# RWKV-7 scan on one core: paired state factors, a block-diagonal state copy, and the inverse scaled on ScalarE

## The chip, the cores and the metric

The program runs on one core of a Trainium2 chip. The metric is the device time of one execution in microseconds. TensorE (PE in the profile, its weight loads PEld) multiplies, VectorE (DVE) and ScalarE (ACT) work on its results, GpSimd (POOL) has little to do here, and SyncE (SP) issues the DMAs. Each engine works through its own instruction queue in order and waits at semaphores for the others.

## The reference, cut to what matters

The program is one layer of a hybrid block: modulated norm, two token mixers side by side (RWKV-7 and GLA), a merge, and a SwiGLU feed-forward part. The change touches the RWKV-7 recurrence alone. It has 16 heads of width 64, 256 context tokens followed by 256 latent tokens, and it runs forward and backward over them; an output is wanted for latent tokens only.

```python
def step(s, inp):                      # s: (heads, v, k), one token
    w_t, k_t, v_t, kk_t, a_t = inp[:5]
    sa = jnp.einsum('bhvk,bhk->bhv', s, kk_t)
    s = (s * w_t[:, :, None, :] - sa[..., None] * (kk_t * a_t)[:, :, None, :]
         + v_t[..., None] * k_t[:, :, None, :])
    return s, jnp.einsum('bhvk,bhk->bhv', s, r_t)     # output, latent tokens only
```

## The kernel before, in words

The scan (phase_rwkv_scan, L1228) works in chunks of C = 64 tokens. There are 8 chunks (NCH) in each of the two directions, and one chunk c in one direction d is called a half here: HALVES lists them as (0,f), (0,b), (1,f), (1,b), and so on, 16 in all, numbered 0 to 15. Halves 0 to 7 are context, 8 to 15 latent. A tile of 128 partitions by 8 pairs (U8) by 64 columns holds all 16 heads, two heads to a pair, one in each half of the partitions.

Within a chunk the recurrence becomes small matrix products per head:

- Decays: a cumulative sum b (DVE, "prepare", L1438), its exponentials es and e2 (ACT, L1543 and L1548), and from them the scaled factors: the two state factors in ldr[:, 1:3] (DVE, "prepare1", L1444), q1 and q2 in q12 (L1452, L1460).
- Scores: products of factors to N (pb, "scores1", L1641), T2 and R2 (pa, L1652), R1 (pb, L1658), each masked on DVE (first L1479, t2r2 L1485, r1 L1490).
- The inverse of (1 - N): five doublings. Each is a DVE transpose (L1463), a DVE mask product (L1465, "step"), an ACT copy ("grown", L1577) and 16 products on PE ("grow", L1694). It ends with "close" (ACT copy L1583, two DVE transposes to "cross" L1499), the product "inverse" (PE L1703), and on DVE L1511, xt = 0.5 * product + half_eye.
- Turning by PE: V to tokens first (L1666, copy vt on ACT L1567), the two state factors (L1666 twice, copies s1t L1571 and s2t L1573).
- own_part (T2 times V, L1711) and rhs_sum (plus q1 times the state S, L1719), copied by ACT (L1587); u = inverse times rhs (L1726, copy L1591).
- Output, latent only: q2 times the state (from_state, L1734), plus R2 times V (L1744), plus R1 times U (L1747).
- State: S + s2^T V + s1^T U (PE L1758 and L1760, 64 x 64 products), added and scaled on DVE (L1519, L1522).

Each fp32 product of the program appears as two matmul records and two weight loads in the trace, so a group of 16 heads is "x32" there. A turning is one record each.

The order on every engine is written out by hand in run(step), L1344. In pass n it interleaves three halves: "now" (half n), "lev" (half n - 1) and "last" (half n - 2). PE's order in a pass is: grow 0 of lev, rhs of last, grow 1, u and from_state of last, grow 2, output and state of last, grow 3, scores of now, grow 4, tokens and flips of now, own_part and inverse of lev; then the next pass. DVE has stage 1 of lev as its first work in a pass, "stage l" being the transpose and mask product after grow l - 1. "prepare" of the half ahead stands at the end of a pass in passes 0 to 7, before own_part and inverse, and in the middle (after stage 3) from pass 8. Passes 16 and 17 only drain.

SP's queue loads ldr (768 KB) and kkv (512 KB) for each half, once q1, b and the second turning of the same direction's last chunk are done.

## Time and profile before

| | us |
|---|---|
| Median of three runs (lowest 2246.99, highest 2255.99) | 2254.05 |
| The profiled execution | 2254.09 |
| Its span | 2252.2 |
| The scan in it: from the first decay sum (978.7) to the last output sum (1285.9) | 307 |
| PE busy over the whole span | 2045.4 (91%) |
| DVE busy | 1363.5 (61%) |
| ACT busy | 789.7 (35%) |

The rest of the program is unchanged work before and after the scan, so the scan is where a difference has to arise. The busy shares are of the whole span; in the scan they are lower for PE and higher for DVE, which the windows below show by pass. In a timeline, each line is an instruction or a merged run of them: its start, its length, engine, line, operation, output and inputs, and in brackets how long the engine had been idle before it and who ended that. "issue" there is idle time of an engine that waited for nothing the profile shows. PEclk is the granted TensorE clock as a share of 2.4 GHz, so 1.00 is 2.4 GHz and 0.50 is 1.2 GHz.

### The profile page before, as it was taken

What the parts mean: (1) busy time and instruction counts of PE and PEld (TensorE: products, weight loads), DVE (VectorE), ACT (ScalarE), POOL (GpSimd) and SP (SyncE); (2) the same over time, 40 slices, a digit from 0 to 9 for tenths busy, and PEclk for the clock granted to TensorE, in tenths of its full rate; (3) what the DMA queues carried; (4) which work ended last, traced back from release to release, by engine and by line L of the source; (5) the groups of instructions that cost most, each with busy time, mean ns of one, the idle gap of its engine ahead of it and who ended that gap; (6) DMA issues with size and microseconds to landing.
All of it is one profiled execution on the core that took longest, in us unless ns stands there. A gap on an engine that the chain in (4) does not pass through costs nothing. (4 is left out here: it accounts for less than half of the span.)

```text
span 2252.2 us, 38698 instructions
## 1 busy us (share of the span) xinstructions
PE 2045.4 (91%) x16787; PEld 1684.7 (75%) x16787; DVE 1363.5 (61%) x1287; ACT 789.7 (35%) x858; POOL 275.8 (12%) x135
## 2 busy tenths in 40 slices
PE   7679999999899989966666799989999999999997
PEld 3268888888589867656666688778888888888886
DVE  3465666665438447768877778466565656554444
ACT  1231111113162225524433365344443434333333
POOL 0242213124105214401000020000000000000000
PEclk9589999999899999988999999999999999999998
DMA  9978888886353378986444187545555555555552
GB/s 334 348 272 327 314 308 305 311 310 181 106 155 103 85 210 260 302 189 171 85 85 87 46 192 260 210 132 179 194 187 194 187 187 186 186 199 193 188 200 97
DMA packets 406151, 454.17 MB, mean 202 GB/s; under 512 B 107550, under 2 KB 356750, under 8 KB 388734
## 3 DMA queue, kind: packets, MB, share of 16 engines
q1 hardware_dynamic: 398400, 441.04, 61.3%
q10 hardware_dynamic: 7614, 11.10, 1.3%
q8 instruction: 110, 1.80, 0.3%
q14 instruction: 27, 0.22, 0.0%
HBM read 413.89 MB, written 38.22 MB: 201 GB/s over the span
## 5 line engine op out<-in xcount | busy, mean ns | idle before, releaser
L215 DVE TENSOR_TENSOR f_w_lo<-t_w_raw,f_w_hi 128x2048 fp32r<-128x2048 f32 x132 | 302.5, 2291 | 307.7 <-ACT f_w_hi L209 307.7
L270 PE MATMUL pf<-h,f_w_hi 128*128 128x512 f32 x1320 | 463.9, 395 | 0.0
L209 ACT ACTIVATE f_w_hi<-t_w_raw 128x2048 fp32r<-128x2048 f32 x132 | 253.4, 1920 | 446.3 <-PE pf L270 283.5
L269 PE MATMUL pf<-h,f_w_lo 128*128 128x256 f32 x1320 | 367.4, 278 | 0.3 <-DVE h L2586 0.3
L270 PEld LDWEIGHTS pf<-h,f_w_hi 128*128 128x128 f32 x1320 | 247.6, 188 | 54.3
L269 PEld LDWEIGHTS pf<-h,f_w_lo 128*128 128x128 f32 x1320 | 248.3, 188 | 4.6 <-DVE h L2586 0.6
L209 ACT ACTIVATE p_w_hi<-h_w_raw 128x2048 fp32r<-128x2048 f32 (+1 forms) x52 | 96.4, 1903 | 340.6 <-DVE stage L726 252.1
L261 PE MATMUL p_in<-h,p_w_lo 128*128 128x512 f32 (+1 forms) x512 | 199.3, 389 | 0.0
L259 PE MATMUL p_in<-h,p_w_hi 128*128 128x512 f32 (+1 forms) x512 | 199.3, 389 | 0.0
L260 PE MATMUL p_in<-h,p_w_hi 128*128 128x512 f32 (+1 forms) x512 | 199.2, 389 | 0.0
L2782 PE MATMUL d_out<-f_w_hi,hid 128*128 128x512 f32 x704 | 178.8, 394 | 6.1 <-DVE f_w_lo L215 6.1
L858 DVE SCALAR_TENSOR_TENSOR late_acc<-h_of_x,siluc,late_acc 128x2048 f32<-128x2048 f32 x60 | 160.6, 2676 | 38.7 <-DMA h_of_x<-in_ada_w 37.1
L215 POOL TENSOR_TENSOR p_w_lo<-h_w_raw,p_w_hi 128x2048 fp32r<-128x2048 f32 (+1 forms) x26 | 123.5, 4752 | 314.3 <-ACT p_w_hi L209 314.3
L2782 PEld LDWEIGHTS d_out<-f_w_hi,hid 128*128 128x128 f32 x704 | 133.7, 190 | 34.9 <-DVE f_w_lo L215 6.9
L904 PE MATMUL po<-h_of_x,gate_w 128*128 128x256 f32 x576 | 132.5, 388 | 2.6 <-DMA gate_w<-in_w_in 1.0
L904 PEld LDWEIGHTS po<-h_of_x,gate_w 128*128 128x128 f32 x576 | 110.6, 195 | 19.7 <-issue 2.5
L261 PEld LDWEIGHTS p_in<-h,p_w_lo 128*128 128x128 f32 (+1 forms) x512 | 95.7, 187 | 20.5
L260 PEld LDWEIGHTS p_in<-h,p_w_hi 128*128 128x128 f32 (+1 forms) x512 | 95.7, 187 | 20.4
L259 PEld LDWEIGHTS p_in<-h,p_w_hi 128*128 128x128 f32 (+1 forms) x512 | 95.7, 187 | 20.4
L270 PE MATMUL p_in<-h,p_w_hi 128*128 128x512 f32 x300 | 108.7, 404 | 0.0
L215 DVE TENSOR_TENSOR m_w_lo<-t_w_raw,h 128x2048 fp32r<-128x2048 f32 x32 | 74.7, 2344 | 45.5 <-ACT h L209 45.4
L904 PE MATMUL r_pg<-h_of_x,gate_w 128*128 128x256 f32 x384 | 90.6, 394 | 11.1 <-PEq L101 6.9
(417 smaller groups left out, 3371.1 us busy)
## 6 DMA issues: line engine op xcount, KB each, us to landing
h_of_x<-in_ada_w SPq DMA_DIRECT2D x64, 1024.0 KB, 5.0
h_w_raw<-in_w_in SPq DMA_DIRECT2D x51, 1024.0 KB, 7.3
t_w_raw<-in_ffn_w_gate SPq DMA_DIRECT2D x44, 1024.0 KB, 5.1
t_w_raw<-in_ffn_w_up SPq DMA_DIRECT2D x44, 1024.0 KB, 5.1
t_w_raw<-in_ffn_w_down SPq DMA_DIRECT2D x44, 1024.0 KB, 4.9
h_w_raw<-in_ada_w SPq DMA_DIRECT2D x32, 1024.0 KB, 8.8
gate_w<-in_w_in SPq DMA_DIRECT2D x32, 1024.0 KB, 5.9
t_w_raw<-in_w_out SPq DMA_DIRECT2D x16, 1024.0 KB, 5.6
```

The source lines that it names most:

```text
L209: act.activation(self.hi[:, m % self.S, 0:w], self.raw[:, s, 0:w], ACT.Copy)\
L215: eng.tensor_tensor(self.lo[:, m % self.S, 0:w], self.raw[:, s, 0:w], b32(self.hi[:, m % self.S, 0:w]), ALU.subtract)\
L259: pe.matmul(o, wh, xh, start=first, stop=False)
L260: pe.matmul(o, wh, xl, start=False, stop=False)
L261: return pe.matmul(o, wl, xh, start=False, stop=last)
L269: pe.matmul(hi, wl, x[:, 0, k, :], start=False, stop=False)
L270: return pe.matmul(both, wh, x[:, :, k, :], start=False, stop=last)
L858: dve.scalar_tensor_tensor(out=acc, in0=self.raw[:, t % 2], scalar=scalar, in1=acc, op0=ALU.mult, op1=ALU.add).then_inc(self.used, 1)
L904: mm = pe.matmul(self.banks[t % nb][:, 0:SEQ], self.raw[:, t % 2, k * P:(k + 1) * P], self.hx[:, k, :], start=k == 0, stop=k == KT - 1)
L2782: return pe.matmul(pd[4 * b + c][:], hid[:, part, t, b * P:(b + 1) * P], v[:, t % 2, 512 * c:512 * c + 512], start=first, stop=stop)
```

## The change

1. **Paired factors.** The two state factors lie side by side as s12 (pair, factor, token), factor order swapped for odd pairs, loaded by two DMAs of their own; the log decays are loaded apart as ld. One turning of a pair's s12 gives both factors with 128 rows: the copy is s21t.
2. **Paired V and U.** One tile vu holds V in one half of the partitions and U in the other (swapped for odd pairs). ACT copies V in two instructions of 64 partitions, and U likewise. The state update is then 16 products with 128 rows instead of 32 with 64.
3. **Block-diagonal state.** Sx is a copy of S with zeros between the two heads of a pair, made by two ACT instructions ("spread"). rhs_sum and from_state are 8 products each on it instead of 16.
4. **Inverse.** PE first writes the identity into pa by two 128 x 256 products (L1742 of after), waits for their end ("ones"), and adds the 16 products onto it; ACT scales by 0.5. The DVE instruction L1511 goes.
5. **A wait in the output.** PE waits for its own R2 V products ("y_own") before the R1 U products.
6. **Order.** In passes 0 to 7 "prepare" of the half ahead now stands behind own_part and inverse; "spread" stands between the copies of stage 4 and close.

Four memory clears on GpSimd instead of two come before the scan. What remains is renaming of operands and places in PSUM.

```diff
+        Sx = pair_of("Sx", [U8, 2, C])
...
+                go("spread", last)
...
+                go("own_part", lev)
+                go("inverse", lev)
                 if not early:
                     go("prepare", ahead)
-                go("own_part", lev)
-                go("inverse", lev)
...
+                    sp.dma_start(ld[d][:], dir_d[d, :, 0:U8, at:at + C]).then_inc(sm("in", d), 16)
+                    for x in range(2):
+                        sp.dma_start(s12[d][:, :, x, :], dir_d[d, :, U8 * (x + 1):U8 * (x + 2), at:at + C])\
+                          .then_inc(sm("in_s", d), 16)
...
+                    dve.wait_ge(sm("in_s", d), c * 32 + 32)
+                    dve.tensor_tensor(s12[d][:], s12[d][:], es[d][:].unsqueeze(2).broadcast_to([P, U8, 2, C]), ALU.mult).then_inc(sm("s12", d), 1)
...
-                def inverse(c, d):
-                    dve.wait_ge(sm("k", d), c + 1)
-                    dve.scalar_tensor_tensor(out=quads(xt[d][:]), in0=narrow(pa[d]), scalar=0.5,
-                                             in1=quads(half_eye[:]), op0=ALU.mult, op1=ALU.add)\
-                       .then_inc(sm("inverse", d), 1)
...
-                    act.activation(quads(vt[d][:]), narrow(pb[d]), ACT.Copy).then_inc(sm("vt", d), 1)
+                    for x in range(2):
+                        act.activation(quads(vu[d][HEAD[x], x]), narrow(pb[d])[HEAD[x]], ACT.Copy).then_inc(sm("vt", d), 1)
...
-                    act.activation(quads(u[d][:]), narrow(pa[d]), ACT.Copy).then_inc(sm("uc", d), 1)
+                    for x in range(2):
+                        act.activation(quads(vu[d][HEAD[1 - x], x]), narrow(pa[d])[HEAD[1 - x]], ACT.Copy).then_inc(sm("uc", d), 1)
+
+                def inverse(c, d):
+                    act.wait_ge(sm("k", d), c + 1)
+                    act.activation(quads(xt[d][:]), narrow(pa[d]), ACT.Copy, scale=0.5).then_inc(sm("inverse", d), 1)
+
+                def spread(c, d):
+                    if c == LAST:
+                        return
+                    act.wait_ge(sm("S", d), c + 1)
+                    for h in range(2):
+                        act.activation(Sx[d][HEAD[h], :, h, :], S[d][HEAD[h]], ACT.Copy).then_inc(sm("spread", d), 1)
...
+                def turn_factors(p, pairs, d):
+
+                    for j in pairs:
+                        at = (j // 2 % 2) * BANK + (j % 2) * P
+                        last = pe.transpose(p[d][:, at:at + P], s12[d][:, j].rearrange("p x c -> p (x c)"), eye[:])
                     return last
...
+                    for b in range(2):
+                        last = pe.matmul(pa[d][:, b * BANK:b * BANK + BANK // 2], eye[:],
+                                         eyes[:, 4 * b:4 * b + 4, :].rearrange("p u c -> p (u c)"), start=True, stop=False,
+                                         skip_group_check=True)
+                    last.then_inc(sm("ones", d), 1)
+                    pe.wait_ge(sm("ones", d), c + 1)
                     of = held(GROW - 1)
                     for j, h in UNITS:
                         last = pe.matmul(placed(GROW)(pa[d], j, h), of(grown[d], j, h), of(cross[d], j, h),
-                                         start=True, stop=True)
+                                         start=False, stop=True, skip_group_check=True)
...
+                        pe.wait_ge(sm("spread", d), c * 2)
                     pe.wait_ge(sm("own", d), c + 1)
-                    for j, h in UNITS:
-                        last = pe.matmul(by_token(pb[d], j, h), feat(q12[d][:, :, 0, :], j, h), feat(S[d], j, h), start=False, stop=True, skip_group_check=True)
+                    for j in range(U8):
+                        last = pe.matmul(in_flips(pb[d], j, 0, j % 2, 2), q12[d][:, j, 0, :], Sx[d][:, j].rearrange("p x c -> p (x c)"),
+                                         start=False, stop=True, skip_group_check=True)
                     last.then_inc(sm("rhs", d), 1)
...
-                        last = pe.matmul(by_feature(pb[d], j, h), feat(S[d], j, h), feat(q12[d][:, :, 1, :], j, h), start=j < 2, stop=False, skip_group_check=True)
+                    for j in range(U8):
+                        at = (j % 2) * BANK + (j // 2) * C
+                        last = pe.matmul(pb[d][:, at:at + C], Sx[d][:, j].rearrange("p x c -> p (x c)"), q12[d][:, j, 1, :],
+                                         start=j < 2, stop=False, skip_group_check=True)
...
+                    last.then_inc(sm("y_own", d), 1)
+                    pe.wait_ge(sm("y_own", d), c - 3)
+                    pe.wait_ge(sm("uc", d), c * 2 + 2)
...
-                    for four in FOURS:
-                        for j, h in four:
-                            pe.matmul(by_feature(pa[d], j, h, 1), flip(s2t[d], j, h), flip(vt[d], j, h), start=True, stop=False)
-                        for j, h in four:
-                            last = pe.matmul(by_feature(pa[d], j, h, 1), flip(s1t[d], j, h), tok(u[d], j, h), start=False, stop=True)
+                    for j in range(U8):
+                        for h in range(2):
+                            last = pe.matmul(by_feature(pa[d], j, h, 1), s21t[d][:, 2 * j + h, :], vu[d][:, j % 2, j // 2 * 2 + h, :],
+                                             start=True, stop=True)
```

Two places in the order are the ones on which the prediction rests. The first is PE from the end of pass 14 (the second turning of half 14's factors) to grow 2 of half 14 in pass 15 ( pa and pb are the PSUM tiles, 0 forward and 1 backward; step and grown belong to the doublings, t2r2 to own_part, cross to the inverse). Before:

```order
L1666 MATMUL pb0<-ident,ldr_f 128x128 x4
L1711 MATMUL pb1<-vt_b,t2r2_b 64x64 x16
L1703 MATMUL pa1<-cross_b,grown_b 64x64 x16
L1694 MATMUL pa0<-first_f,step_f 64x64 x16
L1719 MATMUL pb1<-S_b,q12_b 64x64 x16
L1694 MATMUL pb0<-grown_f,step_f 64x64 x16
L1726 MATMUL pa1<-rhs_b,xt_b 64x64 x16
L1734 MATMUL pb1<-q12_b,S_b 64x64 x16
L1694 MATMUL pa0<-grown_f,step_f 64x64 x16
```

After:

```order
L1706 MATMUL pb0<-ident,s12_f 128x128 x4
L1757 MATMUL pb1<-vu_b,t2r2_b 64x64 x16
L1742 MATMUL pa1<-eyes,ident 128x256 x2
L1749 MATMUL pa1<-cross_b,grown_b 64x64 x16
L1734 MATMUL pa0<-first_f,step_f 64x64 x16
L1766 MATMUL pb1<-Sx_b,q12_b 64x128 x8
L1734 MATMUL pb0<-grown_f,step_f 64x64 x16
L1774 MATMUL pa1<-rhs_b,xt_b 64x64 x16
L1783 MATMUL pb1<-q12_b,Sx_b 128x64 x8
L1734 MATMUL pa0<-grown_f,step_f 64x64 x16
```

The two identity products stand new in front of the inverse, and rhs_sum and from_state have half as many, larger products. The second place is ACT at the end of an odd context pass and the start of the next one. Before:

```order
L1577 ACTIVATE grown_f<-pb0 128x512
L1583 ACTIVATE grown_f<-pa0 128x512
L1567 ACTIVATE vt_b<-pb1 128x512
L1571 ACTIVATE s1t_b<-pa1 128x512
L1573 ACTIVATE s2t_b<-pb1 128x512
L1543 ACTIVATE es_f<-b_f,refs 128x512
L1548 ACTIVATE e2_f<-b_f,refs 128x8x64
L1577 ACTIVATE grown_b<-pa1 128x512
```

After:

```order
L1608 ACTIVATE Sx_b<-S_b 64x8x64 x2
L1588 ACTIVATE grown_f<-pa0 128x512
L1572 ACTIVATE vu_b<-pb1 64x512 x2
L1576 ACTIVATE s21t_b<-pa1 128x512
L1578 ACTIVATE s21t_b<-pb1 128x512
L1601 ACTIVATE xt_f<-pa0 128x512
L1547 ACTIVATE es_f<-b_f,refs 128x512
L1552 ACTIVATE e2_f<-b_f,refs 128x8x64
L1582 ACTIVATE grown_b<-pa1 128x512
```

The spread stands ahead of the copy of close, V's copy is two instructions, and the scaling of the inverse (xt) has come in ahead of the exponentials.

## Rows read from the trace of the kernel before

**Rows 1.** Windows by pass: length, PE, PEld, DVE, ACT, POOL busy, PEclk, DMA, GB/s

```profile
1006.90:1022.10 15.20, 10.67 (x441) 9.11 (x430) 13.57 (x21) 7.08 (x14) 0.00 (x0) 1.00 0.52 97
...
1145.50:1167.10 21.60, 14.50 (x564) 12.97 (x560) 15.84 (x23) 7.69 (x14) 0.00 (x0) 0.92 0.51 92
```

**Rows 2.** Timeline of DVE: stage 1 of pass 8 (no bracket: no idle before it)

```profile
1108.86 0.71 DVE L1463 STREAM_TRANSPOSE turned_b<-pa 128x512 f32<-128x512 f32 x1
```

**Rows 3.** Timeline of PE over the same end of pass 7

```profile
1103.46 0.69 PE L1694 MATMUL pa<-grown_f,step_f 64*64 64x64 f32 x32 [0.41 <-DVE step_f L1465]
1104.20 0.63 PE L1666 MATMUL pb<-ident,kkv_b 128*128 128x128 f32 x4
...
1105.52 0.66 PE L1666 MATMUL pb<-ident,ldr_b 128*128 128x128 f32 x4 [0.18 <-ACT vt_b L1567]
1106.10 1.09 PE L1711 MATMUL pb<-vt_f,t2r_f 64*64 64x64 f32 x30
...
1107.50 0.68 PE L1694 MATMUL pa<-first_b,step_b 64*64 64x64 f32 x31
...
1110.35 0.69 PE L1694 MATMUL pb<-grown_b,step_b 64*64 64x64 f32 x32 [1.70 <-DVE step_b L1465]
```

**Rows 4.** Timeline of ACT over the same stretch

```profile
1104.86 0.60 ACT L1567 ACTIVATE vt_b<-pb 128x512 f32<-128x512 f32 x1
1105.37 0.60 ACT L1571 ACTIVATE s1t_b<-pa 128x512 f32<-128x512 f32 x1
...
1108.40 0.72 ACT L1543 ACTIVATE es_f<-b_f,refs 128x512 f32<-128x512 f32 x1 [1.59 <-DVE b_f L1438]
```

**Rows 5.** Timeline of DVE, end of pass 14 and into pass 15

```profile
1249.56 0.69 DVE L1511 SCALAR_TENSOR_TENSOR xt_b<-pa,half_eye 128x512 f32<-128x512 f32 x1 [1.16 <-PE pa L1703]
1250.17 0.71 DVE L1463 STREAM_TRANSPOSE turned_f<-pa 128x512 f32<-128x512 f32 x1
...
1255.02 0.72 DVE L1463 STREAM_TRANSPOSE turned_f<-pa 128x512 f32<-128x512 f32 x1 [0.28 <-PE pa L1694]
```

**Rows 6.** Timeline of PE over the same stretch

```profile
1247.28 0.65 PE L1666 MATMUL pb<-ident,ldr_f 128*128 128x128 f32 x4 [0.25 <-ACT vt_f L1567]
...
1249.26 0.68 PE L1694 MATMUL pa<-first_f,step_f 64*64 64x64 f32 x31
...
1253.24 1.10 PE L1734 MATMUL pb<-q_b,S_b 64*64 64x64 f32 x32
1254.19 0.69 PE L1694 MATMUL pa<-grown_f,step_f 64*64 64x64 f32 x32
```

**Rows 7.** Timelines elsewhere, and PE's groups over the scan (busy, mean ns)

```profile
50.42 0.97 PEld L455 LDWEIGHTS p_col<-sel,ada_rows 128*128 128x128 f32 x8 [1.30 <-DVE ada_rows L534]
...
990.13 1.99 PE L904 MATMUL pb<-h_of_x,gate_w 128*128 128x256 f32 x8
992.06 0.69 PE L1694 MATMUL pb<-grown_f,step_f 64*64 64x64 f32 x32
...
L904 PE MATMUL pb<-h_of_x,gate_w 128*128 128x256 f32 x60 | 14.9, 400 | 0.0
```

**Rows 8.** PE's timeline, idle ended by "issue": the first, the longest, the last

```profile
1012.00 0.39 PE L1694 MATMUL pa<-grown_b,step_b 64*64 64x64 f32 x10 [0.56 <-issue]
...
1036.56 0.90 PE L1666 MATMUL pb<-ident,kkv_b 128*128 128x128 f32 x3 [2.88 <-issue]
...
1259.34 0.63 PE L1694 MATMUL pb<-grown_f,step_f 64*64 64x64 f32 x28 [1.41 <-issue]
```

**Rows 9.** PE late in pass 17; first DVE work of the scan

```profile
1284.00 0.69 PE L1744 MATMUL pb<-t2r_b,vt_b 64*64 64x64 f32 x32 [0.17 <-PE pb L1734]
...
978.74 1.22 DVE L1438 TENSOR_TENSOR_SCAN b_f<-keep,ldr_f 128x512 f32<-128x512 f32 x1 [1.49 <-DMA ldr_f<-rwkv_dir_scratch]
```

**Rows 10.** DVE's groups over the scan: busy, mean ns, idle before

```profile
L1511 DVE SCALAR_TENSOR_TENSOR xt_f<-pa,half_eye 128x512 f32<-128x512 f32 x8 | 5.5, 682 | 7.0 <-PE pa L1703 7.0
L1511 DVE SCALAR_TENSOR_TENSOR xt_b<-pa,half_eye 128x512 f32<-128x512 f32 x8 | 5.5, 682 | 4.8 <-PE pa L1703 4.8
```

87 lines of the change are left out of this document (49 added, 38 removed).

## The prediction

> **What bounds the kernel now.** Only the scan's code changes, so I read the windows of its passes first, then the timelines of DVE, PE and ACT over a clean context pass and a clean latent one, then PE's idle time.
>
> By the windows a pass takes 15.2 us where nothing goes wrong and up to 21.6 us [rows 1]. In the clean one DVE is busy 13.6 of 15.2 us, in the long one 15.8 of 21.6. So two things make a pass: a DVE queue that is nearly full, and stalls that lengthen passes with hardly more DVE work. The doublings tie DVE to PE: each transpose waits for a group of products, each group for a mask product.
>
> What the reader should see at the end of pass 7: DVE enters stage 1 of pass 8 with no gap [rows 2]; the decay sum and xt filled the time before it. PE's last group before it, grow 0, starts at 1107.50 and ends at 1108.18 [rows 3], so it is ready 0.68 us before DVE takes it at 1108.86. That 0.68 us is PE's only slack there. At the end of pass 14 no decay sum covers the wait: DVE is idle 1.16 us for the inverse product, does xt, and takes grow 0 (ended 1249.94) at 1250.17 [rows 5, 6]. PE is in one piece before that: turnings, own_part, inverse, grow 0. So at the end of every pass PE's chain is the bound or within 0.7 us of it.
>
> The stalls: PE's timeline has 27 gaps of 0.48 us or more that end with "issue", from 1012.00 to 1259.34, the longest 2.88 us, 35.4 us together [rows 8]. They fall inside groups of equal products, where no semaphore is awaited; I read them as late instructions.
>
> **The change part by part.** The sum is made against the profiled execution, 2254.09 us, which is the median of the runs to 0.04 us.
>
> *Taken from DVE.* xt goes: 0.61 us from start to start [rows 5], in 16 passes, with the wait ahead of it. By itself this lets DVE reach stage 1 earlier, but there it waits for grow 0. Hence the ends of passes are costed on PE's side.
>
> *V's copy in two.* The second turning waits for vt (0.18 and 0.25 us of idle already, [rows 3, 6]). An ACT copy takes 0.51 us from start to start (1104.86 to 1105.37, [rows 4]) for 512 columns; half the partitions leaves the columns as they are, so I count another 0.5 us on PE's chain. Bounds 0.3 to 0.6.
>
> *The identity products.* Two fp32 products of 128 x 256 are four records. Eight such take 1.93 us from the first start to the next group's [rows 7], 0.24 each, and one lasts 0.40 us. Three starts and the whole last one are 0.72 + 0.40 = 1.12 us. Then PE waits for its own semaphore: 0.17 us, as in the one row where it now does so [rows 9]. Ahead of them PE goes from 64-row to 128-row products: in pass 7 the turnings start 0.74 us after grow 4 [rows 3], where a group issues in 0.47 to 0.5, so 0.2 us. Sum 1.5 us, all ahead of inverse and grow 0; bounds 1.1 to 1.8. The Trainium skill, TensorEngine Tiling (Array Packing), section Tiling Modes, says that changing the tiling mode drains the TensorE; the 0.74 us agree.
>
> *The end of a pass.* PE's chain grows by 2.0 us. Latent (passes 8 to 15): stage 1 began 0.23 us after grow 0 ended; without xt it can begin after some 0.09. So 2.0 - 0.14 = 1.86 us, eight times: 14.9. Context (passes 1 to 7): the slack of 0.68, less 0.07, is used up first, 1.4 us remain. ACT adds to that: its scaling of the inverse now stands ahead of es and e2. Moved by 2.0 us, the inverse ends near 1109.7, scaling at 0.5, two exponentials at some 0.65 (each is 0.72 long, [rows 4]) and the copy of stage 1 at 0.6 follow, 2.4 us, so grow 1 starts some 0.5 us later than its mask product would allow; prepare1 on DVE covers about 0.3 of it. The spread (two ACT instructions of 512 columns, about 1.0 us in a gap of about 0.9) adds 0.1. So 1.7 us, seven times: 11.9. Pass 0 has no inverse, only V's copy: 0.5. Together 27.3.
>
> *from_state.* Eight products with the full 128 x 128 array of weights and 64 columns are 16 weight loads. Eight full loads with two columns each span 0.97 us [rows 7], 0.12 each, so the load is the price: 1.9 us, and 0.3 for the two changes of mode, 2.2 against 0.95 now (1253.24 to 1254.19, [rows 6]). grow 2 follows at once and DVE is already idle for it (0.28, [rows 5]), so 1.2 us show, in passes 10 to 16: 8.4. Bounds 0 (loads hidden) and 1.5 each.
>
> *rhs_sum.* 16 records of 128 columns, 0.9 us if the two column halves run beside each other and 1.8 if not, against 0.47. After grow 0 PE has 1.70 us of idle behind it [rows 3], so nothing, or 0.2 in the worse case.
>
> *The state update.* 32 records on 128 rows instead of 64 on 64. 64 records at the pace of the groups above are 2 x 0.47 us, four quarters of the array at work. With the two column halves side by side it is again 0.95, one after another 1.9. In latent passes the decay sum and q2 cover either. In context passes the DVE sum follows stage 3 closely; U's second copy (0.5) ahead of it gives 0 to 0.8 us, seven times, I take 1.0 in all. On this the skill says two things: TensorEngine Tiling, section Tiling Modes, lets different tiles load and multiply in parallel; TensorE: Matmul & The Clock Gate, Part 3, lets a weight load overlap a running matmul only if the row groups differ, and all of these use all rows. No row here shows column halves alone. By the first the state is free, by the second it costs some 5 us.
>
> *The output's wait.* y_own: a group lasts 0.69 and issues in 0.47, so 0.22 us for the last product's end, and 0.17 [rows 9], 0.4 us; covered where DVE has the decay sum, seen in passes 14 and 15 where DVE waits for y: 0.8.
>
> *The start and the end.* The first decay sum waits 1.49 us for ldr [rows 9]; ld is a third of it, so 1.4 us are gained (bounds 0 and 1.5). The two larger clears on GpSimd are over before that. Passes 16 and 17 have no cover: identity 1.5, rhs 0.4, from_state 1.3, y_own 0.4 = 3.6.
>
> *Nothing.* prepare1 has the same 1024 columns. The loads move the same bytes, and s12 is wanted a whole stage after ld. Moving "prepare" behind the inverse matters only on ACT, counted above.
>
> Added: 27.3 + 8.4 + 1.0 + 0.8 + 3.6 - 1.4 = **39.7 us**, bounds 28 and 48.
>
> *Stalls given back.* PE has 768 fewer of 7744 matmul records in the scan, 10%, and 17% fewer in the stretch from grow 1 to grow 3 (240 for 288 in a latent pass, 160 for 192 in a context one), where most stalls fall. They are also spread over a longer time: 240 records in about 7.5 us instead of 288 in about 5.5. What the stalls cost today is bounded by the passes: against 15.2 us for a context pass, and about 17.9 for a latent one with output (its 15.8 of DVE work and the clean idle times), the passes from 3 to 15 are 29 us too long. Between 10% (the share of records) and 90% of that comes back; I take half, **14.5 us**, since the demand per microsecond falls by a third.
>
> Net 39.7 - 14.5 = 25.2: **2279 us**.
>
> **The rivals.**
>
> 1. *The forecast:* PE's chain at the end of each pass sets the time, half the stalls go. 2279.
> 2. *The stalls were the real bound.* They nearly all go (-26), and loads hide (+32): 2260. For it: 27 gaps in 300 us. Against it: the clean pass 7 end has none and its chain still grows. The result would be within 0.5%.
> 3. *Little comes back and the column halves do not overlap.* Added 46, given back 5: 2295. For it: the gaps lie wherever the loads' bursts fall, which do not change.
> 4. *Faster:* DVE's queue is the bound and PE hides its additions. One mechanism: the identity products run while PE would wait anyway, between own_part and the end of close. Then xt (0.61 in 16 passes) and its waits (7.0 and 4.8 us, [rows 10]) go, 21 us, plus 14 of stalls, less 12 for from_state and the end: 2231. It decides once PE's added chain is under 0.6 us in context and 0.1 in latent passes. Against: cross is ready before own_part is done, so PE has no wait there [rows 3, 6].
> 5. *It does not do what it says:* the 128-row products are fewer but take PE longer. That is already in the sum; it is why nothing is credited for them but stalls.
>
> **How the numbers follow.** The first case 0.55, the second 0.18, the third 0.18, the fourth 0.09. What a measurement of this kernel can tell from no change is about 0.5%, 11 us. The first case lies above 2265.3 with most of its weight (its own range 2266 to 2292), the third wholly, the second mostly within. Slower by over 0.5%: 0.50 + 0.18 + 0.03 = 0.71; within: 0.05 + 0.14 = 0.19; faster: 0.10. The range takes in the second case and most of the third: 2256 to 2297.
>
> **What would show it.** In the trace after: DVE idle before stage 1 of each pass, 1.5 to 3 us, ended by grow 0; 1.3 to 1.7 us between own_part's end and the first inverse product; from_state near 2 us and DVE idle over 1 us before stage 3 in latent passes; clean context passes near 17 us; fewer and shorter "issue" gaps. The forecast is wrong if the inverse starts within 0.5 us of own_part, if a lower granted clock appears where PE waits, or if the gaps do not shrink.

## The result and the profile after

The changed kernel takes 2264.05 us (median of 5 runs, 2260.12 to 2267.83), the kernel before 2254.05 (2246.99 to 2255.99). The ratio is 1.0048, 95% interval 1.0024 to 1.0071: slower by 10 us, where 25 were forecast. The profiled execution of after took 2260.12 us with a span of 2258.3, so the two traces differ by 6.1 us. It is these that are taken apart here; the traced execution of after is the lowest of its five, so by the medians every account below has 4 us less given back.

Most of what the forecast put on PE's chain is there. The end of pass 7 and the end of pass 14 in the timeline of PE, after (start, length, group, idle before and what ended it); compare [rows 3, 6]:

```profile
1105.65 0.66 PE L1706 MATMUL pb<-ident,s_b 128*128 128x128 f32 x4 [0.91 <-ACT vu_b L1572]
...
1246.67 0.66 PE L1706 MATMUL pb<-ident,s_f 128*128 128x128 f32 x4 [0.86 <-ACT vu_f L1572]
1247.25 1.15 PE L1757 MATMUL pb<-vu_b,t2r_b 64*64 64x64 f32 x32
1248.33 1.13 PE L1742 MATMUL pa<-eyes,ident 128*128 128x256 f32 x4
1249.52 0.69 PE L1749 MATMUL pa<-cross_b,grown_b 64*64 64x64 f32 x32
1250.04 0.65 PE L1734 MATMUL pa<-first_f,step_f 64*64 64x64 f32 x32
1250.61 1.09 PE L1766 MATMUL pb<-Sx_b,q_b 128*64 128x128 f32 x16
```

The second turning waits 0.86 us for V's copy, where it waited 0.25. From own_part's start to the inverse's it is 1249.52 - 1247.25 = 2.27 us, with the identity products between them; from own_part's end it is 1.1 us, where 1.3 to 1.7 were to be seen. DVE shows the sum of it, in its timeline at the ends of passes 7 and 13, and in its groups over the scan (last two rows: busy, mean ns | idle before):

```profile
1109.80 0.72 DVE L1473 STREAM_TRANSPOSE turned_b<-pa 128x512 f32<-128x512 f32 x1 [1.76 <-PE pa L1734]
...
1229.98 0.72 DVE L1473 STREAM_TRANSPOSE turned_b<-pa 128x512 f32<-128x512 f32 x1 [3.62 <-PE pa L1734]
...
1235.82 0.72 DVE L1473 STREAM_TRANSPOSE turned_b<-pa 128x512 f32<-128x512 f32 x1 [1.31 <-PE pa L1734]
```

```profile
L1473 DVE STREAM_TRANSPOSE turned_f<-pa 128x512 f32<-128x512 f32 x16 | 11.5, 717 | 29.7 <-PE pa L1734 29.7
L1473 DVE STREAM_TRANSPOSE turned_b<-pa 128x512 f32<-128x512 f32 x16 | 11.5, 717 | 30.8 <-PE pa L1734 30.8
```

Stage 1 of a pass now waits 1.76 us in context and 3.62 in latent passes, stage 3 waits 1.31, where [rows 2, 5] had no gap, none (behind xt) and 0.28. Together DVE waits 60 us for grow 0 and grow 2.

The products of 128 rows in one latent pass, PE's timeline of after:

```profile
1233.06 2.00 PE L1783 MATMUL pb<-q_f,Sx_f 128*128 128x64 f32 x16
1234.99 0.69 PE L1734 MATMUL pa<-grown_b,step_b 64*64 64x64 f32 x32
1235.51 0.65 PE L1794 MATMUL pb<-t2r_f,vu_f 64*64 64x64 f32 x32
1236.64 0.69 PE L1799 MATMUL pb<-r_f,vu_f 64*64 64x64 f32 x32 [0.49 <-PE pb L1794]
1237.26 1.15 PE L1811 MATMUL pa<-vu_f,s21t_f 128*64 128x64 f32 x32
1238.35 0.69 PE L1734 MATMUL pb<-grown_b,step_b 64*64 64x64 f32 x32
```

from_state issues in 1.93 us (1233.06 to 1234.99), the output's wait for y_own is 0.49 us, and the state update takes 1238.35 - 1237.26 = 1.09 us for 32 records: the two column halves do run beside each other.

What did not go by the forecast is the other side. After has 13 gaps of PE ended by "issue" of 0.2 us or more, 9.8 us together, where before has 27 with 35.4 us [rows 8]. The first and longest of them, and one of the latent passes, in PE's timeline of after:

```profile
1034.58 0.34 PE L1685 MATMUL pa<-q_b,s_b 64*64 64x64 f32 x6 [2.51 <-issue]
...
1195.91 0.46 PE L1794 MATMUL pb<-t2r_f,vu_f 64*64 64x64 f32 x16 [0.75 <-issue]
```

And the granted clock is whole. The windows over most of the latent passes, 1127 to 1268 us, before and then after (length, PE, PEld, DVE, ACT, POOL busy, PEclk, DMA share, GB/s):

```profile
1127.00:1268.00 141.00, 98.89 (x3774) 89.38 (x3778) 108.42 (x154) 51.36 (x93) 0.00 (x0) 0.92 0.36 68
```

```profile
1127.00:1268.00 141.00, 110.31 (x3392) 94.49 (x3392) 103.94 (x148) 72.83 (x128) 0.00 (x0) 1.00 0.37 70
```

PE is busy 110 us of 141, where it was busy 99, and at full clock (2.4 GHz) throughout. The passes of after are more alike: the common context pass takes 16.41 us, the common latent one 20.37, where before had 15.2 to 20.2 and 17.3 to 21.9. "Clean" below is the shortest common length.

### The profile page after: what moved, and what is told of

It is laid out like the page before. It is cut to its first block and busy times, and to the rows that moved or that the text cites. A ratio compares the mean times of both kernels' runs of the same rounds, so it can differ in the third digit from the quotient of the medians.

```text
span 2258.3 us, 37280 instructions
## 1 busy us (share of the span) xinstructions
PE 2065.3 (91%) x16019; PEld 1692.2 (75%) x16019; DVE 1352.4 (60%) x1271; ACT 834.6 (37%) x934; POOL 277.1 (12%) x137
```

## The experiments

All were compared with the kernel before on their own chip, where its median was 2251.3 to 2254.4 us; a difference to before is read from the ratio. "Gaps" is the sum of PE's idle times of over 0.15 us ended by "issue" in one profiled execution; "pace" is the scan's matmul records divided by the scan's length without those gaps, worked out from the timelines. (The pace contains the gaps in its divisor, so the two columns are not independent; with the whole scan as divisor the correlation of the first 13 rows is 0.79, as printed 0.92.)

The pace is a rough guide and no more. b_half_state and b_identity have the same pace (27.4 and 27.3) and gaps of 35.4 and 24.9 us; by the whole scan before and b_identity are equal (25.2 and 25.1 records per us), with 35.6 and 24.9 us. Each sum of gaps is of one execution, and how much it differs between executions of one kernel was not measured.

| kernel | us | ratio to before (95%) | gaps us | pace, records per us |
|---|---|---|---|---|
| before | 2254 | 1 | 35.6 | 7744 / 271.6 = 28.5 |
| b_fs128 | 2253.09 | 1.0009 (0.9986 to 1.0033) | 33.9 | 27.8 |
| b_half_state | 2247.82 | 0.9969 (0.9956 to 0.9982) | 35.4 | 27.4 |
| b_identity | 2254.13 | 1.0008 (0.9994 to 1.0021) | 24.9 | 27.3 |
| best1 | 2237.62 | 0.9927 (0.9908 to 0.9947) | 24.3 | 27.1 |
| b_pad | 2267.77 | 1.0061 (1.0037 to 1.0085) | 26.4 | 26.9 |
| state128 | 2244.78 | 0.9961 (0.9939 to 0.9984) | 27.2 | 26.6 |
| b_dvelong | 2270.30 | 1.0083 (1.0056 to 1.0110) | 22.1 | 25.3 |
| a_dveown_fs64 | 2247.31 | 0.9982 (0.9961 to 1.0002) | 27.1 | 25.1 |
| a_dveown | 2244.33 | 0.9963 (0.9940 to 0.9987) | 18.4 | 24.5 |
| a_fs64 | 2261.86 | 1.0046 (1.0013 to 1.0079) | 15.3 | 23.5 |
| a_dveinv | 2247.97 | 0.9971 (0.9958 to 0.9985) | 9.7 | 23.2 |
| after | 2264.05 | 1.0048 (1.0024 to 1.0071) | 9.8 | 6976 / 306.4 = 22.8 |
| b_waits | 2338.08 | 1.0387 (1.0362 to 1.0412) | 5.4 | 7744 / 388.2 = 19.9 |
| b_long_runs | 2253.95 | 1.0005 (0.9990 to 1.0021) | 35.3 | 7744 / 269.3 = 28.8 |

**b_identity**: before, with the new inverse alone: the identity products, ScalarE's scaling, and "prepare" behind them.

```diff
+                    for b in range(2):
+                        last = pe.matmul(pa[d][:, b * BANK:b * BANK + BANK // 2], eye[:], ...)
+                    pe.wait_ge(sm("ones", d), c + 1)
-                    dve.scalar_tensor_tensor(out=quads(xt[d][:]), in0=narrow(pa[d]), scalar=0.5, ...)
+                    act.activation(quads(xt[d][:]), narrow(pa[d]), ACT.Copy, scale=0.5)
```

> The kernel before with one part of the change: PE writes the identity into pa by two 128 x 256 products and waits for them, the 16 products of the inverse are added onto it, ScalarE scales by 0.5, and prepare stands behind own_part and inverse. 64 matmul records more, nothing else moved. In the trace of after, this piece took 1.39 us on PE (2.27 us from own_part's start to the inverse's, against 0.88 before). Theory A, PE's chain at the end of a pass is the bound and late instructions come of demand per microsecond: the eight latent pass ends grow by 1.25 us, the seven context ones by some 0.9, the end by 1.4, +18 us, and part of the 29 us of stalls comes back, so 2258 to 2266, with fewer gaps ended by issue than the 27 of before. Theory B, late instructions come of the number of records: the gaps stay at 30 to 36 us in sum and the time is 2270 to 2274. Theory C, VectorE's queue is the bound: 2245 or less, since it loses 0.61 us in each pass.

Measured: no change. DVE's idle time before stage 1 rose to 1.3 us in clean context and some 3.0 us in latent passes, so the chain did grow; xt left DVE, and the gaps shrank by 11 us. The parts cancel.

**a_dveinv**: after, with that one part undone (its edit against after).

```diff
-                    act.activation(quads(xt[d][:]), narrow(pa[d]), ACT.Copy, scale=0.5)
+                    dve.scalar_tensor_tensor(out=quads(xt[d][:]), in0=narrow(pa[d]), scalar=0.5, ...)
-                        last = pe.matmul(pa[d][:, b * BANK:b * BANK + BANK // 2], eye[:], ...)
-                go("own_part", lev)
-                go("inverse", lev)
                 if not early:
                     go("prepare", ahead)
+                go("own_part", lev)
+                go("inverse", lev)
```

> The changed kernel with the inverse as before: no identity products, no wait for them, VectorE scales and adds half the identity, prepare ahead of own_part. Everything else of the change stays. Theory A (PE's chain bounds the pass ends): 1.39 us off each of them where it shows, 16 to 19 us less than the changed kernel, 2245 to 2250, thus faster than the kernel before by 0.2 to 0.4%; idle time of VectorE before stage 1 near 0 in context passes, and about 1.7 us before xt in latent ones. Theory C (VectorE's queue): slower than the changed kernel by up to 10 us. Should the stalls have gone because these products spread PE's work over time, some of the 25 us of gaps return and the time is 2255 or more.

Measured: 16 us less than after, and faster than before. The clean context pass goes from 16.41 to 14.81 us, latent ones from 20.37 to 19 to 20. In after, then, the new inverse (identity products, scaling on ScalarE, order of "prepare") costs 1.6 and about 1 us a pass, and it is not what removed the gaps: those stay at 9.7 us. In before, by b_identity, the same part costs nothing in net: what a part costs depends on the gaps beside it.

**b_half_state**: before, with 448 records fewer.

```diff
-                            pe.matmul(by_feature(pa[d], j, h, 1), flip(s2t[d], j, h), flip(vt[d], j, h), start=True, stop=False)
-                        for j, h in four:
-                            last = pe.matmul(by_feature(pa[d], j, h, 1), flip(s1t[d], j, h), tok(u[d], j, h), start=False, stop=True)
+                            last = pe.matmul(by_feature(pa[d], j, h, 1), flip(s2t[d], j, h), flip(vt[d], j, h), start=True, stop=True)
```

> The kernel before with the second half of the state update left out (s1 times U is not added; 16 of 32 products, 448 matmul records fewer in the scan), so the state is incomplete. No other engine has less to do, and PE's chain at the end of a pass is the same. It asks whether the number of PE instructions alone moves the stalls. If late instructions cost by demand between grow 1 and grow 3, 8 to 15 us of the 29 come back: 2240 to 2246, and the gaps ended by issue sum to 15 to 25 us instead of 35. If the stalls are an accident of the loads' bursts: 2250 to 2256, gaps as before.

Measured: 6 us faster, gaps unchanged at 35.4 us. Fewer records by themselves do not shrink the gaps: the scan became shorter with them. The thought in the forecast's rival 2, that stalls go with the records, fails in that form.

**b_long_runs**: before, with the passes' loads in runs of 2 KB.

```diff
-                    sp.dma_start(ldr[d][:].rearrange("p a u t -> p (a u) t"), dir_d[d, :, :, at:at + C])\
+                    sp.dma_start(ldr[d][:].rearrange("p a u t -> p a (u t)"), dir_d[d].rearrange("p (a u) t -> p a u t", a=3)[:, :, c, :])\
```

> The kernel before with other data loaded: each load of factors and of keys and values takes the 512 tokens of one pair, one run of 2 KB per partition and kind, in place of 64 tokens of eight pairs in runs of 256 bytes. The bytes and every instruction on the engines stay; the tokens scanned are others. It asks whether PE's instructions are late because their fetch stands behind the scan's many small packets. If so, the gaps ended by issue fall from 35 us to under 10 and the time to 2225 to 2235. If the fetch is slow by itself: gaps 30 us or more, 2250 to 2256.

Measured: nothing, in time or gaps (35.3 us), though the DMA share from 990 to 1285 us fell from 0.45 to 0.29. The small size of the loads' packets is not the cause. The loads' bytes and their times stayed, so this run does not clear the loads themselves.

**state128**: only the state update in its new form, with the paired factors and V and U in two copies. A part of its edit against after:

```diff
-                        last = pe.matmul(in_flips(pb[d], j, 0, j % 2, 2), q12[d][:, j, 0, :], Sx[d][:, j].rearrange("p x c -> p (x c)"), ...)
+                        last = pe.matmul(by_token(pb[d], j, h), feat(q12[d][:, :, 0, :], j, h), feat(S[d], j, h), ...)
-                        last = pe.matmul(pb[d][:, at:at + C], Sx[d][:, j].rearrange("p x c -> p (x c)"), q12[d][:, j, 1, :], ...)
+                        last = pe.matmul(by_feature(pb[d], j, h), feat(S[d], j, h), feat(q12[d][:, :, 1, :], j, h), ...)
```

> The kernel after with its inverse on DVE again and without Sx: rhs_sum, from_state and own_part are the 64 x 64 groups of before (with V taken from vu), and only the state update runs as 32 records on 128 rows, with the paired factors and V and U in two copies each. Theory R (the late instructions come where records are asked for fastest, and 64 x 64 groups ask fastest; slow 128-row products let the supply catch up): two thirds of the slow products are gone again, so the gaps lie between the two kernels, 18 to 30 us against 35 of before and 10 of the form with Sx and the inverse on DVE; from_state is 1.0 us again (7 x 1.2 = 8 us less than that form) and 8 to 20 us of gaps come back: 2246 to 2256 us. Theory S (the paired state update alone is what removes the gaps, 64 records in 0.95 us becoming 32 in 1.1): gaps near 10 us, 2236 to 2242 us. Theory N (the number of records): 448 fewer records did not change the gaps before, so 35 us and 2258 to 2264 us.

Measured: 2244.78 us, 1 us below theory R's range, and gaps of 27.2 us, within it; theory S and theory N are out. It has as many records as b_half_state (7296) in a scan as long (301.7 and 302.0 us), but 8 us fewer gaps; its 32 state records are spread over 1.09 us instead of being 32 fast ones. (Its lower pace comes from the gaps in the divisor alone.) This part of the change alone is a gain of 0.4%.

**b_fs128**: before, with Sx and from_state on 128 rows alone.

```diff
+                    pe.wait_ge(sm("spread", d), c * 2)
-                    for j, h in UNITS:
-                        last = pe.matmul(by_feature(pb[d], j, h), feat(S[d], j, h), feat(q12[d][:, :, 1, :], j, h), ...)
+                    for j in range(U8):
+                        last = pe.matmul(pb[d][:, at:at + C], Sx[d][:, j].rearrange("p x c -> p (x c)"), q12[d][:, j, 1, :], ...)
```

> The kernel before, with Sx and its two copies by ScalarE, used by from_state alone: 16 records of 128 x 128 weights in about 2.0 us instead of 32 of 64 x 64 in about 1.0, in latent passes. Nothing else is changed. Cost by the chain alone: 1.0 us in passes 10 to 16 and at the end, 8 to 9 us, 2262 us. Theory R (demand per microsecond): gaps in the latent passes (about 20 of the 35 us) fall by a third to a half, 7 to 10 us back, 2252 to 2256 us. Theory N or S (number of records, or the state update): gaps stay at 33 to 37 us, 2260 to 2264 us.

Measured: 2253.09 us, within theory R's time, but the gaps hardly fell (33.9 us), which was expected of theory N. What paid for the 8 us of slower products is not settled. They do show: DVE's idle time before stage 3 is 1.29 us in the clean latent passes, as in after, where before has 0.28. Yet the latent passes took 157.6 us against 159.4. A miss for both theories in part.

**b_pad**: before, with 16 slow records more per pass.

```diff
+                    for j in range(U8):
+                        last = pe.matmul(pb[d][:, at:at + C], eye[:], eye[:, 0:C], start=True, stop=True)
+                    last.then_inc(sm("pad", d), 1)
+                    pe.wait_ge(sm("pad", d), c + 1)
```

> The kernel before with eight fp32 products of a 128 x 128 identity by 64 columns put ahead of from_state in every pass (their output is written over and never read) and one wait of PE for them: 16 more records per pass, 256 in all, slow ones of 0.12 us each, and 2.1 us more on PE's queue. By the chain alone each pass from 1 on is up to 2.1 us longer where DVE waits for grow 2 (some 1.5 us after the slack): 2254 + 16 x 1.5 = 2278 us. Theory R (demand per microsecond): more records but more time for them, gaps fall to 10 to 20 us, and the granted clock rises from 0.91 to over 0.95: 2258 to 2268 us. Theory N (number of records): gaps stay at 35 us or grow, 2275 to 2290 us.

Measured: 256 records more and 9 us fewer gaps (26.4; theory R had 10 to 20), at 2268 us, the upper edge of theory R, and the granted clock from 990 to 1285 us at 0.95 where before has 0.91. That is a miss for theory R's gaps; but more records with fewer gaps put the number of records out as a cause. PE's queue grew by up to 33 us (16 x 2.1), of which 24 were expected to show; the time grew by 14 to 16.

**a_dveown**: a_dveinv, with own_part ahead of the turnings of s1 and s2 on PE.

```diff
                 go("tokens", now)
+                go("own_part", lev)
                 go("flips", now)
-                go("own_part", lev)
                 go("inverse", lev)
```

> The kernel after with the inverse on DVE (no identity products) and own_part on PE moved ahead of the turnings of s1 and s2, so that it runs before grow 0's inputs are wanted and the second turning has its copy of V ready. Theory of the chain (PE's queue of turnings, own_part, inverse, grow 0 sets the end of each pass, and V's copy in two stalls the second turning for 0.86 us): own_part fills that stall, each pass end is 0.5 to 0.9 us shorter than in the form with the inverse on DVE, 15 x 0.6 = 9 us: 2236 to 2243 us. If DVE's queue or the wait for cross bounds the end instead: 2246 to 2250 us, no change from that form.

Measured: the wait for V's copy is gone, and clean latent passes fall from about 19.1 to 18.2 us. But context passes stay at 14.8, DVE having no idle time before stage 1 there, and 9 us of gaps come back. In net 2244 us, above the 2236 to 2243 that the chain alone gave: 2 us less than a_dveinv by the ratios, 4 by the medians, where 9 were expected. PE's timeline at the end of a latent pass:

```profile
1219.07 1.15 PE L1754 MATMUL pb<-vu_f,t2r_f 64*64 64x64 f32 x32
1220.15 0.66 PE L1709 MATMUL pa<-ident,s_b 128*128 128x128 f32 x4
1220.64 0.60 PE L1709 MATMUL pb<-ident,s_b 128*128 128x128 f32 x4
1221.17 0.69 PE L1746 MATMUL pa<-cross_f,grown_f 64*64 64x64 f32 x32
```

**b_dvelong**: the test of a slower pace with PE's program left as it is. DVE is given 1.8 us more at each pass end.

```diff
+                    for n in range(3):
+                        dve.scalar_tensor_tensor(out=spare[:, n], in0=half_eye[:], scalar=0.5,
+                                                 in1=half_eye[:], op0=ALU.mult, op1=ALU.add)
```

> The kernel before with three more operations of 512 columns on DVE behind the inverse (xt) of each pass, written to a spare tile that nobody reads: no record of PE is added, taken or changed, but each pass end is 3 x 0.6 = 1.8 us longer, 16 x 1.8 = 29 us. Theory D (late instructions follow how many records PE is asked for per microsecond of the scan, its gaps left out: 7744 / 271.8 = 28.5 before with 35.4 us of gaps, 6976 / 306.4 = 22.8 after with 9.8, and the seven experiments between them in line): 7744 / 301 = 25.7, so gaps of 20 to 24 us and 11 to 15 us given back, in net 2254 + 29 - 13 = 2270 us (2266 to 2274), and the granted clock above before's 0.91. Theory F (the form of the 128-row products matters, not the demand): gaps stay at 33 to 37 us, the clock stays or falls, 2280 to 2286 us.

Measured: 2270.3 us and 22.1 us of gaps, both as theory D had them. The added work in DVE's timeline, and what PE waits for longest from 990 to 1285 us (us in total, times, longest):

```profile
1242.57 1.89 DVE L1516 SCALAR_TENSOR_TENSOR spare<-half_eye 128x512 f32<-128x512 f32 x3
```

```profile
PE pb L1698 <- DVE step_b L1466: 23.2, 9, 3.5
PE pb L1698 <- DVE step_f L1466: 20.6, 9, 3.5
```

Against before on the same chip (2251.31 us) the time grew by 19 us (13 to 25 by the interval), between the two traces by 17. So 29 us put on the chain cost 17 to 19, and the other ten or twelve were paid for by late instructions that were no longer late: the gaps fell by 13. One part of the expectation failed: the granted clock did not rise. It is 0.88 from 990 to 1285 us, against 0.91 before. Fewer gaps alone do not bring the clock back. Nor does PE's busy time tell the clock: over that window it is 225 us at 0.99 in after and 208 at 0.91 in before, but 203 at 0.94 in b_long_runs and 256 at 0.87 in b_waits. Why after has the full clock is open.

**a_fs64**: after, with from_state as 64 x 64 products on S.

```diff
-                        last = pe.matmul(pb[d][:, at:at + C], Sx[d][:, j].rearrange("p x c -> p (x c)"), q12[d][:, j, 1, :], ...)
+                        last = pe.matmul(by_feature(pb[d], j, h), feat(S[d], j, h), feat(q12[d][:, :, 1, :], j, h), ...)
```

> The kernel after with from_state alone as 32 records of 64 x 64 weights on S again, in place of 16 with 128 x 128 weights on Sx. By the chain alone grow 2 comes 1.0 to 1.2 us sooner in passes 10 to 17: 9 us less, 2255 us. By theory D the demand rises to 7104 / 297.5 = 23.9 records per microsecond and 3 to 6 us of gaps come back: 2257 to 2261 us, gaps 12 to 17 us. If gaps do not follow demand: 2253 to 2256 us with gaps of 8 to 11 us.

Measured: 2261.86 us (2250.65 to 2273.02), gaps 15.3 us, as theory D had the gaps. Taking 9 us off the chain gained 2 us by the medians and under 1 by the ratios, but five runs that scatter over 22 us do not settle it.

**best1**: state128 with own_part ahead of the turnings (its edit against state128).

```diff
                 go("tokens", now)
+                go("own_part", lev)
                 go("flips", now)
...
-                go("own_part", lev)
                 go("inverse", lev)
```

> Only the state update as 128-row products, inverse on DVE, no Sx, and own_part ahead of the turnings of s1 and s2, so that the second turning does not wait for V's second copy. Chain: 0.3 to 0.6 us less at each pass end than without the move of own_part (15 x 0.45 = 7 us). Theory D: demand rises from 26.6 to 27.2 records per microsecond, 2 to 4 us of gaps come back, in net 2239 to 2243 us. Theory of a full DVE queue: nothing moves, 2243 to 2247 us.

Measured: 2237.62 us, 0.7% faster than before and the fastest of all: 7 us less than state128, slightly more than expected. The gaps are a miss for theory D: the pace rose from 26.6 to 27.1, yet they fell by 3 us (27.2 to 24.3) where 2 to 4 us were to come back.

**a_dveown_fs64**: a_dveown, with the edit of a_fs64.

```diff
-                    for j in range(U8):
-                        last = pe.matmul(pb[d][:, at:at + C], Sx[d][:, j].rearrange("p x c -> p (x c)"), q12[d][:, j, 1, :], ...)
+                    for j, h in UNITS:
+                        last = pe.matmul(by_feature(pb[d], j, h), feat(S[d], j, h), feat(q12[d][:, :, 1, :], j, h), ...)
```

> The form with the inverse on DVE and own_part ahead of the turnings (2244.3 us, 18.4 us of gaps at 24.5 records per microsecond), with from_state as 64 x 64 products on S again; rhs_sum keeps Sx. Chain: 9 us less. Theory D: 7040 / 273 = 25.8 records per microsecond, gaps 21 to 25 us, 3 to 6 us back: 2237 to 2242 us. Without theory D: 2234 to 2237 us.

Measured: 2247 us (2239.8 to 2257.15, 12 runs), a miss. The gaps came back by 9 us, and the granted clock over 990 to 1285 us fell from 0.95 to 0.92, so that nothing is left of the 9 us of chain. Why it lost more than the pace explains (27.1 us at 25.1 records per us) is open; 22.8 of its 27.1 us lie where the scan's loads run (see the next section).

**b_waits**: before, with two waits more ahead of each product of the doublings.

```diff
                     for j, h in UNITS:
+                        for n in range(2):
+                            pe.wait_ge(sm("step", d), c * GROW + (l + 1))
```

> The kernel before with two more waits of PE ahead of each product of the doublings (grow), on a count that has long been reached: nothing is computed, moved or awaited more, but PE's instruction stream is 80 to 160 instructions longer per pass. Theory I (late instructions are late 16 KB blocks of PE's instruction stream: the page of before has the instruction queue's packets at 16 KB each, 54 of them in the 262 us in which PE shows 6876 records, 127 records each, and the gaps lie 126 or 127 records or a multiple of that apart): there are more than 54 such packets for the same work (57 to 63), gaps that follow one another come less than 126 records apart where grow lies between them, the gaps sum to more than 35 us (38 to 55) and the time is 2256 to 2275 us, more if each wait also costs PE time to issue. Theory T (the gaps count records of products or some event of time, such as the loads): the packets may grow, but gaps stay 126 or 127 records apart, 33 to 37 us, and the time stays within 2248 to 2258 us.

Measured: the time says nothing on either theory, because one wait of the two is an instruction of its own that costs PE 0.1 us to issue: the totals of the profile's pages are 38698 and 39978 instructions, 1280 = 80 groups of 16, and a group takes 2.2 us where it took 0.69. PE's timeline of b_waits:

```profile
1213.61 2.19 PE L1696 MATMUL pa<-grown_b,step_b 64*64 64x64 f32 x32
```

The rest tells more. The instruction queue's row on the page, before and then b_waits (packets, MB, share):

```profile
q8 instruction: 110, 1.80, 0.3%
```

```profile
q8 instruction: 115, 1.88, 0.3%
```

Five packets more for 1280 instructions: a packet is 256 instructions, 16 KB. And two gaps that follow one another, in PE's timeline:

```profile
1252.08 0.56 PE L1736 MATMUL pb<-q_f,S_f 64*64 64x64 f32 x10 [0.78 <-issue]
1252.47 2.27 PE L1696 MATMUL pa<-grown_b,step_b 64*64 64x64 f32 x32
...
1256.38 0.27 PE L1762 MATMUL pa<-u_f,s1t_f 64*64 64x64 f32 x2 [0.43 <-issue]
```

Between them lie 118 records with one group of grow, not 126 or 127: 236 instructions, the 16 added waits, and a few waits besides. That is theory I's sign, and theory T is out. With a longer stream, but asked for at 19.9 records per us, the gaps nearly vanish: five of 0.2 us or more, 4.5 us, where theory I had 38 to 55 (the six of 0.15 us that make it 5.4 in the table stand at other distances and may be the waits themselves).

## What the late instructions are

In the window 1006 to 1268 us the instruction queue brought, before and then after:

```profile
q8 instruction: 54, 0.88, 1.4%
```

```profile
q8 instruction: 48, 0.79, 1.3%
```

PE has 6876 matmul records there in before and 6109 in after: 127 records per packet in both. With its weight load each record is two instructions, so a packet holds about 127 records and a few waits. And the gaps lie 126 or 127 records apart, or a multiple of that. PE's timeline of before over one stretch; between the first two rows lie 32 records each of grow, u_step and from_state and 10 of the next grow, so 21 + 96 + 10 = 127, and the third gap comes another 127 later:

```profile
1209.70 0.57 PE L1719 MATMUL pb<-S_b,q_b 64*64 64x64 f32 x21 [0.68 <-issue]
...
1216.29 0.51 PE L1694 MATMUL pa<-grown_f,step_f 64*64 64x64 f32 x19 [2.85 <-issue]
...
1219.69 0.28 PE L1760 MATMUL pa<-u_b,s1t_b 64*64 64x64 f32 x4 [1.32 <-issue]
```

The same gaps stand at the same record in another program with the same instructions so far. One more gap of before, beside the longest of [rows 8], and then both in b_fs128, whose scan began 3.4 us earlier:

```profile
1098.66 0.34 PE L1694 MATMUL pa<-grown_f,step_f 64*64 64x64 f32 x5 [2.11 <-issue]
```

```profile
1032.49 0.90 PE L1675 MATMUL pb<-ident,kkv_b 128*128 128x128 f32 x3 [3.10 <-issue]
...
1095.25 0.33 PE L1703 MATMUL pa<-grown_f,step_f 64*64 64x64 f32 x5 [2.11 <-issue]
```

So PE waits at the border of a block of 256 instructions. The packets themselves show it: in the 15 traces every one of the 295 gaps of 0.2 us or more ends 1.2 to 1.7 us after the end of a 16 KB packet of the instruction queue. Here are the two stretches of before between the three rows above, 127 records each (length, PE, PEld, DVE, ACT, POOL busy, PEclk, DMA share, GB/s):

```profile
1209.70:1216.29 6.59, 3.50 (x128) 3.23 (x127) 3.78 (x6) 2.24 (x4) 0.00 (x0) 1.00 1.14 188
1216.29:1219.69 3.40, 2.08 (x127) 1.95 (x127) 2.67 (x4) 0.69 (x2) 0.00 (x0) 1.00 0.02 5
```

In the second the DMA engines are idle but for the instructions. The packet starts at 1217.50, 1.2 us after PE passed the border, takes 0.9 us, and PE goes on 1.3 us after its end: 3.4 us, the shortest time between two gaps at neighbouring borders in any of the traces, while 127 records of the 64 x 64 groups issue in about 2 us (0.47 to 0.5 per 32). In the first the scan's loads are running (the share adds up the packets' own times, so it can pass 1). The packet starts at 1213.40, 3.7 us after the border, takes 1.3, and PE goes on after 1.6 more: 6.6 us, where PE had work for 3.7.

The loads matter in all the traces. With the borders between two gaps put in at equal distances in records (an estimate), there are 241 stretches of a block in which the DMA share was over 0.6, in the 14 kernels other than b_waits: 150 ended with a gap, and those took 6.1 us on average. Of the 338 with a share under 0.1, 88 did, and took 3.9 us. Of the stretches in which PE had work for 3.5 to 5 us, 81 of 124 were late with the loads running and 19 of 147 without. So a late block is one that PE was through with before the next had come; a slower PE gives it time, and the loads take time from it. In before 23.9 of the 35.4 us lie where the loads run, in b_dvelong 8.0 and in after 6.9, while the rest is 11.5, 13.9 and 2.9: it is mostly the gaps beside the loads that the longer passes removed. That the loads cause the delay is not shown by a run of its own: b_long_runs changed the size of their packets, and none has fewer loads or moves them.

The Trainium skill, Runtime: NRT & Kernel Launch, section Instruction fetch mechanics, says that PE's instructions are refilled in blocks of 256, over a DMA queue of its own, at a cost that is mostly hidden. The block size agrees with the 16 KB packets and the 127 records; that it is hidden does not: 35.4 us of 307 in the scan of before.

## Why the prediction was off

Right, by its own steps (forecast, then measured):

- V's copy in two: 0.5 us on the chain; the second turning waits 0.6 us longer (0.86 for 0.25).
- Identity products: 1.5; own_part to inverse went from 0.88 to 2.27, 1.4.
- from_state: 2.2 with its changes of mode; 1.93. DVE waits 1.31 us before stage 3 where it waited 0.28, so 1.0 shows instead of 1.2.
- State update: no more than before. The column halves overlap: 1.09 us for the 32 records, where the forecast had 0.95 side by side and 1.9 one after another. rhs_sum's 16 records of 128 columns last 1.09 us too (0.9 was said). The rule of the Trainium skill by which it would have cost 5 us (TensorE: Matmul & The Clock Gate, Part 3) did not hold here; that of TensorEngine Tiling (Array Packing), section Tiling Modes, did.
- The end: 3.6; 21.32 - 17.62 = 3.7.

Wrong, in the additions:

- *The end of a pass*, context: 1.7 each, 11.9. The clean pass grew from 15.22 to 16.41, 1.2 each, 8.3. Which part of the 1.7 did not show was not separated.
- Latent: 24.1 with from_state and y_own. The clean pass is 20.37 against 17.9, 2.5 each, 20. That 17.9 was the forecast's own estimate, and no latent pass of before is free of gaps, so this term is the least sure.
- *The start*: -1.4. The decay sum did begin sooner (975.65 for 978.74), yet DVE came to the first stage 1 at 990.42, as before at 990.34. The 0.5 of pass 0 lies ahead of that and is in this sum. PE's timeline after, with [rows 7] for comparison, and the window of it:

```profile
981.10 0.69 PE L1674 MATMUL pb<-s_f,q_f 64*64 64x64 f32 x32 [3.09 <-DVE q_f L1462]
...
986.09 3.57 PE L904 MATMUL pb<-h_of_x,gate_w 128*128 128x256 f32 x8
```

```profile
985.00:992.00 7.00, 6.82 (x52) 5.27 (x52) 2.25 (x4) 3.13 (x6) 0.00 (x0) 0.68 0.78 149
```

The eight gate products ahead of grow 0 took 3.57 us, where such eight take 1.99 [rows 7], and the granted clock was 0.68. PE had waited 3.09 us for q before that; in before it had waited 2.62 at the same place, behind more gate products, and kept the full clock. What tipped it is not settled, but the sooner start was lost in slower products: 0 gained. A lower clock where PE waits was one of the forecast's own signs of being wrong; it came true here.

The additions sum to 8.3 + 20 + 3.7 + 0 = 32 us, where 39.7 were forecast.

**The step that failed is "Stalls given back".** The traces differ by 6.1 us, so 32 - 6.1 = 26 us came back, not 14.5 (22 by the medians). Of the 19 us by which the forecast was off, this step has 11 to 12 and the additions 7 to 8. The mechanism was named, and the size was chosen as half of 29, with 90% of it, 26, as the upper bound. Two things were missed. The forecast began with what the change takes from PE's records (10%), but b_half_state shows that this alone gives nothing back. And it counted the slower demand from grow 1 to grow 3 only: that its own 32 us of longer passes give every block more time stands nowhere in the sum. b_dvelong has that effect alone, with 10 to 12 us given back for 29 added. From 28.5 to 22.8 records per us the gaps went from 35.6 to 9.8 us, a difference of 25.8, close to the 26; how much more than b_dvelong's share the new products give is not separated.

The time was nearly rival 2's outcome (2260, a chance of 0.18), whose terms were +32 and -26. One of them came out for a wrong reason: it took 32 because the weight loads of from_state would hide, and they did not (1.93 us). That is luck. And the stalls were not the bound instead of the chain: a longer chain and the late blocks fill the same time. Rival 3's remark that the gaps lie where the loads' bursts fall was right for two thirds of before's gaps; that they would therefore stay was not.

The clock is a second part of a gap's price, and the forecast had none of it. In best1 one gap in PE's timeline, and the windows ahead of it, behind it and after that, show this:

```profile
1208.05 1.46 PE L1797 MATMUL pa<-vu_b,s21t_b 128*64 128x64 f32 x25 [2.22 <-issue]
1209.44 1.13 PE L1728 MATMUL pb<-grown_f,step_f 64*64 64x64 f32 x32
```

```profile
1203.00:1205.80 2.80, 2.71 (x126) 2.39 (x124) 2.30 (x5) 1.96 (x4) 0.00 (x0) 1.00 0.97 201
1208.00:1212.00 4.00, 3.95 (x109) 3.83 (x113) 2.39 (x4) 1.37 (x4) 0.00 (x0) 0.57 0.03 6
1213.00:1217.00 4.00, 3.37 (x105) 3.02 (x106) 3.67 (x6) 1.78 (x3) 0.00 (x0) 1.00 0.00 0
```

After a gap of 2.22 us the granted clock was 0.57 for 4 us, close to the lower level of 1.2 GHz, and a doubling group took 1.13 us where it takes 0.69. It is not so after every gap: behind the 2.85 us of before the clock was 1.00 up to 1219.6 and 0.74 from 1220 to 1224. How much of the 26 us is gaps and how much clock was not separated. b_long_runs comes nearest, with 0.94 for 0.91 at the same gaps: its median is that of before, its traced execution 6 us shorter.

## What to carry to other kernels

Idle time of TensorE that ends with "issue", at equal distances in records, was here a late block of its instruction stream. It comes where PE runs through 127 fast products in less time than a block takes to come, which was 3.4 us with the DMA engines idle and 6 us beside the scan's loads. The number of instructions does not tell it, and the mean pace only roughly. In such a kernel work added to the chain costs less than it adds (b_dvelong 17 to 19 us of 29), and work taken off can gain less (a_dveown_fs64 nothing of 9); so cost the gaps again at the new pace before summing. And take a change in several parts apart: here the paired state update alone, with own_part moved into the wait for V's copy, makes the kernel 0.7% faster, while the new inverse costs 16 us in after and nothing in before.

## What was not expected of the hardware

- PE's blocks of 256 instructions (16 KB, 127 products with their weight loads) came late by up to 3.83 us (b_dvelong, at 1034.27), and late ones followed each other at 3.4 us or more. A packet of the instruction queue starts 1.2 us after PE passed a border with the DMA engines idle, and 3.2 us after it with a DMA share over 0.6 (medians of the late ones).
- A wait that was met long ago, as an instruction of its own, takes PE 0.1 us: 16 of them made a group of 0.69 us one of 2.2.
- Products of 128 rows on the two column halves overlap: 32 records of 128 x 64 weights issue in 1.09 us, 34 ns each, while 16 of 128 x 128 take 1.93 us, 121 ns each.
- PE's wait for its own last product was 0.49 us here (y_own), where [rows 9] had 0.17.
